# Two transformer blocks in one kernel: unread products in TensorE's waits, norm steps in another order, x loaded first

## The reference, cut to what matters

```python
for l in range(2):
    h = rms_norm(x, norm_mix[l])
    x = x + (short_conv_mixer(h, ...) if l == 0 else moba_attention(h, ...))
    x = x + mem_cross_attention(rms_norm(x, norm_mem[l]), rms_norm(mem, norm_memkv[l]), ...)
    x = x + swiglu(rms_norm(x, norm_ffn[l]), ffn_w_gu[l], ffn_w_down[l])
x = rms_norm(x, norm_final)
# second block
sh1, sc1, gt1, sh2, sc2, gt2 = split(silu(c) @ w_mod + b_mod)
h = rms_norm(x, g_mix) * (1 + sc1) + sh1
proj = h @ w_in          # gated delta net branch and latent attention branch
x = x + gt1 * (merged @ w_out)
h = rms_norm(x, g_ffn) * (1 + sc2) + sh2
x = x + gt2 * expert_choice_ffn(h, ...)   # 16 experts
out = rms_norm(x, g_final)
```

## Time and profile before

| what | value |
|---|---|
| runs | 1796.09, 1805.71 and 1807.78 us, median 1805.71 |
| profiled execution | 1801.72 us, its span 1800.0 us |
| TensorE busy | 1580.0 us (88%), 14736 products |
| VectorE, ScalarE, GpSimd busy | 868.8, 666.6, 145.5 us |
| mean PEclk | 0.93 |
| data moved by DMA | 417.17 MB |

### The profile page before, as it was taken

How to read it: one execution, slowest core, us unless ns; L and a number is a source line. 1 busy time by engine, 2 the same in 40 slices (tenths; PEclk the granted TensorE clock), 3 DMA queues, 4 the chain that set the end, 5 groups by cost and what they waited for, 6 DMA issues and landing times.

```text
span 1800.0 us, 35085 instructions
## 1 busy us (share of the span) xinstructions
PE 1580.0 (88%) x14736; PEld 1308.6 (73%) x14736; DVE 868.8 (48%) x1228; ACT 666.6 (37%) x869; POOL 145.5 (8%) x188
## 2 busy tenths in 40 slices
PE   7999999999999999999889799899898676666667
PEld 7999899988979889988888699698884232222223
DVE  4765466646565556664567588956541000000001
ACT  5445355434544445534465745524431000000001
POOL 5800000000000000000105002131010000000000
PEclk9999999999999999999899899999999677776789
DMA  7765656764736666755353154002779999999997
GB/s 240 237 211 188 187 161 190 236 244 152 258 114 219 197 185 188 195 173 192 102 165 94 55 164 135 26 27 95 275 290 402 421 421 421 421 421 421 420 421 306
DMA packets 254142, 417.17 MB, mean 232 GB/s; under 512 B 15103, under 2 KB 215346, under 8 KB 229426
## 3 DMA queue, kind: packets, MB, share of 16 engines
q1 hardware_dynamic: 252833, 411.96, 64.2%
q10 hardware_dynamic: 1168, 3.17, 0.5%
HBM read 414.04 MB, written 1.05 MB: 231 GB/s over the span
## 4 chain that ended last, share of the span: by engine, by line
issue 60%; PE 28%; DVE 4%; POOL 4%; ACT 3%; DMA 1%; DVEq 0%; POOLq 0%; ACTq 0%; SPq 0%
PE bank L417 3%; PE bank L418 3%; PE bank L419 3%; PE bank L1819 2%; PE bank L434 1%; PE bank L435 1%; PE bank L436 1%; PE bank L1036 1%; PE bank L1038 1%; POOL ang L867 1%; PE bank L1037 1%; DVE cy L1368 1%; ACT w_hi L243 1%; POOL ang L868 1%; PE bank L472 0%
## 5 line engine op out<-in xcount | busy, mean ns | idle before, releaser
L250 DVE TENSOR_TENSOR w_lo<-w_raw,w_hi 128x2048 fp32r<-128x2048 f32 (+2 forms) x178 | 401.5, 2258 | 258.0 <-ACT w_hi L243 257.9
L243 ACT ACTIVATE w_hi<-w_raw 128x2048 fp32r<-128x2048 f32 (+2 forms) x178 | 334.2, 1881 | 152.1 <-DMA w_raw<-in_ffn_w_down_dram 61.6
L417 PE MATMUL bank<-h_hi,w_hi 128*128 128x256 f32 x1168 | 327.5, 280 | 5.2 <-DVE h_lo L632 3.5
L418 PE MATMUL bank<-h_lo,w_hi 128*128 128x256 f32 x1168 | 325.8, 279 | 0.0
L419 PE MATMUL bank<-h_hi,w_lo 128*128 128x256 f32 x1168 | 325.6, 279 | 0.0
L2614 PE MATMUL bank<-w_exp,xeT 128*32 128x256 f32 x2048 | 174.3, 479 | 84.0 <-DMA w_exp<-in_w_up_dram 47.9
L417 PEld LDWEIGHTS bank<-h_hi,w_hi 128*128 128x128 f32 x1168 | 222.0, 190 | 7.0 <-issue 4.5
L419 PEld LDWEIGHTS bank<-h_hi,w_lo 128*128 128x128 f32 x1168 | 222.1, 190 | 0.0
L418 PEld LDWEIGHTS bank<-h_lo,w_hi 128*128 128x128 f32 x1168 | 221.7, 190 | 0.0
L2614 PEld LDWEIGHTS bank<-w_exp,xeT 128*32 128x32 f32 x2048 | 66.0, 129 | 185.2 <-DMA w_exp<-in_w_up_dram 83.3
L2782 DVE TENSOR_TENSOR hx<-sg,bank 128x256 f32<-128x256 f32 x16 | 6.7, 421 | 279.2 <-ACT sg L2756 279.2
(11 more groups left out here) (531 smaller groups left out, 3085.3 us busy)
## 6 DMA issues: line engine op xcount, KB each, us to landing
w_exp<-in_w_gate_dram SPq DMA_DIRECT2D x64, 1024.0 KB, 26.7
w_exp<-in_w_up_dram SPq DMA_DIRECT2D x64, 1024.0 KB, 26.9
w_exp<-in_w_down_dram SPq DMA_DIRECT2D x64, 1024.0 KB, 26.9
w_raw<-in_ffn_w_gu_dram SPq DMA_DIRECT2D x88, 512.0 KB, 5.0
w_raw<-in_w_in_dram SPq DMA_DIRECT2D x54, 512.0 KB, 4.7
w_mod<-in_w_mod_dram SPq DMA_DIRECT2D x24, 1024.0 KB, 7.6
w_raw<-in_ffn_w_down_dram SPq DMA_DIRECT2D x44, 512.0 KB, 4.3
w_raw<-in_mem_w_kv_dram SPq DMA_DIRECT2D x32, 512.0 KB, 4.7
```

The costliest lines, as they stand in the source:

```text
L243: e.activation(whi[slot][:, 0:w], raw[slot][:, 0:w], ACT.Copy).then_inc(S["hi_ready"], 1)
L250: e.tensor_tensor(wlo[slot][:, 0:w], raw[slot][:, 0:w], whi[slot][:, 0:w].bitcast(F32), ALU.subtract).then_inc(S["lo_ready"], 1)
L417: e.matmul(dst, whi[slot][:, lo:hi_], bh[:, k, :], start=(k == 0), stop=False)
L418: e.matmul(dst, whi[slot][:, lo:hi_], bl[:, k, :], start=False, stop=False)
```

## The change

- x is loaded by SP ahead of the first weights, not by ACT.
- The gains norm_mix are turned and copied ahead of the norm of x, not behind its transposes.
- Unread products are added to TensorE's list: 8 and 12 of the identity with itself around the turning of the gains, 5 behind the transposes of x, and 32 at the seam. Nothing reads their results.
- `fm_chunk`, in a chunk that waits for tiles, goes by tile k and takes both halves f for each, with one start for the bank.
- `load_late` goes from ACT's list to SP's, behind the sixth chunk of ffn(1).
- At the seam: sums are joined in another way (squares are scaled by 1/D as they are taken, the square of x of the last bank moves from VectorE to ScalarE and that of xn from ScalarE to VectorE), nrow is scaled in halves of 512 columns and the first eight transposes wait for the first halves only, and `split_biased` replaces the loop with two buffers by four buffers in x and another order of steps.

```diff
     def fm_chunk(bh, bl, width=256, kts=KT):
+        fs = width // P
         def chunk(e, c, u, slot):
-            for f in range(width // P):
+            by_tile = st.tiles is not None
+            for f, k in ([(f, k) for k in range(kts) for f in range(fs)] if by_tile else
+                         [(f, k) for f in range(fs) for k in range(kts)]):
                 dst = G[u][:, f * SEQ:(f + 1) * SEQ]
-                for k in range(kts):
-                    if f == 0:
-                        wait_tile(e, k)
...
+                begin = k == 0 and (f == 0 or not by_tile)
+                end = k == kts - 1 and (f == fs - 1 or not by_tile)
...
-    act.raw(load_x)
+    sp.raw(load_x)
...
+    def unread_identity(n):
+        def run(e):
+            e.wait_ge(*t_id)
+            for _ in range(n):
+                e.matmul(G[2][:, 0:P], ident[:, :], ident[:, :], start=True, stop=True)
+        pe.raw(run)
+    unread_identity(8)
+    t = pe.do(lambda e: e.transpose(G[3][:, 0:16], vrow[0:16, 0, :], ident[0:16, 0:16]), (mix_in, 16), t_id)
+    t_gain = dve.do(lambda e: e.tensor_copy(vcol[:, 0:16], G[3][:, 0:16]), t)
+    unread_identity(12)
     rows = norm_rows(x, [(x_in, 16)])
     first_split(0)
     turned = turn_rows(xn, rows)
-    t = pe.do(lambda e: e.transpose(G[3][:, 0:16], vrow[0:16, 0, :], ident[0:16, 0:16]), (mix_in, 16), t_id)
-    t_gain = dve.do(lambda e: e.tensor_copy(vcol[:, 0:16], G[3][:, 0:16]), t)
-    th = split_features(turned, lambda k: col("norm_mix", k), None, [t_gain])
+    unread_identity(5)
+    th = split_features(turned, lambda k: col("norm_mix", k), [t_gain])
     first_split(1)
...
         gemm(FT, source, fm_chunk(h_hi, h_lo), act_chunk=act_silu, dve_chunk=dve_gate, dve_links=2,
-             ready=[tx], act_ready=[tx], dve_ready=[tx])
+             ready=[tx], act_ready=[tx], dve_ready=[tx], beside={5: load_late} if l else None)
...
-    act.raw(load_late)
...
+    def split_biased(toks, gain, bias, free, whole):
...
+        by_dve(0)
+        by_dve(2)
+        hi(0)
+        by_act(1)
+        hi(1)
+        hi(2)
+        by_act(3)
+        hi(3)
+        for j in range(KT // 2):
+            tl = dve.do(lambda e, j=j: e.tensor_tensor(
+                h_lo[:, 2 * j:2 * j + 2, :], whole[:, j, :, :], h_hi[:, 2 * j:2 * j + 2, :].bitcast(F32), ALU.subtract), hi_at[j])
...
+    def unread_at_seam(n):
+        w = xfree[3]
+        def run(e):
+            e.wait_ge(*w)
+            for _ in range(n):
+                e.matmul(X[3][:, 0:SEQ], a_hi[:, 0, 0:P], a_hi[:, 1, :], start=True, stop=True)
+        pe.raw(run)
+    unread_at_seam(32)
```

More of the change, by code:

```diff
@@ L618, in turn_rows, with split_features @@
         return toks
-    def split_features(toks, gain, bias, free, also=(), into=None, behind=None, whole=None):
+    def split_features(toks, gain, free, into=None, behind=None):
         tls = []
@@ L625, in split_features @@
             tp = toks[j]
[L626 to L651, removed]
+            pair = [(2 * j + kk, X[j][:, kk * SEQ:(kk + 1) * SEQ]) for kk in range(2)]
+            for k, xj in pair:
+                th = act.do(lambda e, k=k, xj=xj: e.activation(to_hi[:, k, :], xj, ACT.Copy, scale=gain(k)),
+                            tp, *free, *([behind[k]] if behind else []))
+            for k, xj in pair:
+                tl = dve.do(lambda e, k=k, xj=xj: e.scalar_tensor_tensor(
+                    out=to_lo[:, k, :], in0=xj, scalar=gain(k), in1=to_hi[:, k, :].bitcast(F32),
+                    op0=ALU.mult, op1=ALU.subtract), th)
+            xfree[j] = tl
             tls += [tl, tl]
@@ L661, in norm_to_features @@
                 modulate(vector, j)
-        return split_features(turn_rows(xn, rows), gain, bias, free, whole=whole)
+        return split_features(turn_rows(xn, rows), gain, free)
     def attention(heads, kts, scale, score, v, pbuf, ptbuf, ready, causal=None, free=(), vector=None, beside=None):
@@ L1096, in build @@
     turned = turn_rows(xn, rows)
-    th = split_features(turned, lambda k: col("kv_norm", k), None, [all_used()])
-    th2 = split_features(turned, lambda k: col("norm_mix", 8 + k), None, [all_used()], into=h2,
+    th = split_features(turned, lambda k: col("kv_norm", k), [all_used()])
+    th2 = split_features(turned, lambda k: col("norm_mix", 8 + k), [all_used()], into=h2,
                          behind=tiles_of[th])
@@ new lines, in build @@
+    scaled = {}
+    for hf in range(2):
+        hs = slice(hf * BANK, (hf + 1) * BANK)
+        t0 = dve.do(lambda e, hs=hs: e.tensor_scalar(nrow[:, 0, hs], xn[:, 0, hs], roots[:, 2:3], None, ALU.mult), t_roots)
+        t1 = act.do(lambda e, hs=hs: e.activation(nrow[:, 1, hs], xn[:, 1, hs], ACT.Copy, scale=roots[:, 3:4]), t_roots)
+        scaled[2 * hf] = scaled[2 * hf + 1] = [t0, t1]
+    turned = turn_rows(nrow, [], by_pair=scaled)
+    ht4 = x[:, :, :].rearrange("p t d -> p (t d)").rearrange("p (j a t) -> p j a t", j=4, a=2)
@@ L1253, in build @@
+    th = split_biased(turned, lambda k: mcol[:, 1, k:k + 1], lambda k: mcol[:, 0, k:k + 1], [tcol, all_used()], ht4)
     dve.raw(lambda e, m=st.n + AHEAD - 1: lo_split(e, m, m % RING))
```

72 lines of the change are left out of this document (43 added, 29 removed).

## The result

The changed kernel takes 1798.3 us, median of 22 runs (1790.34 to 1803.29). The kernel before, run beside it, takes 1805.76, median of 22 (1796.09 to 1813.57). The ratio is 0.996, with a 95% interval of 0.9948 to 0.9972: 5.1 to 9.4 us are won. The forecast was 1791.5 with 14.2 won. So the direction is right, the time lies inside the range, and the size is about half of what was forecast.

A forecast was written before the change was run, and what follows sets the result against it. TensorE was taken to bound the first 1280 us, expert weights the span from 1360 on. Terms 4.8 + 3.8 + 5.4 + 0.2 = 14.2 off the median 1805.71 gave 1791.5, with 8 in 10 in 1782 to 1800.

The forecast's parts named there:

- The start, 4.8: Program start: x 1.2 earlier, gains 1.1 sooner, 2.5 from the clock held up; 4.8 us won, bounds 1.1 and 5.0.
- The clock was taken as 2.5: First chunk at the start: unread products keep TensorE at full clock, winning the 2.5 us between first and second chunk.
- the first rival, "the clock is down": Start and seam: both first products at 1.2 GHz; only 9.5 won, 1796.2; chance 0.27 with cases of only one down.
- Into ffn(1), 3.8: Entry of ffn(1): load_late off ScalarE's queue wins 2.9, no slow first products 0.9; 3.8 us, bounds 2.9 and 3.8.
- I cost it at nothing; the cover is these 6.7: Seventh weight chunk of ffn(1), behind the late loads on SP's queue: 6.7 us spare, so the delay costs nothing.
- Rival 3: ffn(1): broadcast loads, 8.0 each in a row, hold the weight queue; 17.3 stop, 3.1 slower, 1808.8; chance 0.03.
- its own counterargument: Against the held weight queue in ffn(1): the broadcasts' 8.0 us landings ran side by side, with weights beside them.
- The seam, 5.4: Between the blocks: less idle, faster transposes, first product 1.0 sooner, no 1.34 stop; 5.4 us won, bounds 1.0 and 5.6.
- By tile elsewhere, 0.2: Chunks outside start and seam: waits for low parts leave at most 0.6 between pairs; 0.2 us taken as won.
- rival 2: First block: the start's gain is lost there, VectorE hardly pausing between 70 and 100 us; 9.4 won, 1796.3; chance 0.08.

The follow-up runs named there:

- e2: Changed kernel with 12 unread products instead of 5 behind the first 16 transposes; 1790.62 in one run (before 1799.35).
- e4: Changed kernel with the five late loads spread behind chunks 5, 8, 11 and 14 of ffn(1); 1801.15 in one run (before 1799.35).
- e8: Changed kernel with late loads spread over ffn(1) and 12 unread products instead of 5 ahead of the first product; 1799.2, ratio 0.9968.
- e3: Changed kernel without the 32 unread products at the seam; 1796.67 in one run (before 1799.35).
- e5: Changed kernel with the chunks of products by output half again, not by tile; 1798.11, ratio 0.9969.
- f1: Kernel before with only the five late loads moved to SP's queue behind chunk 5 of ffn(1); 1802.31, ratio 0.9999.
- e6: Changed kernel with the five late loads on ScalarE's queue again, ahead of its norm in ffn(1); 1798.17, ratio 0.996.
- e7: Changed kernel with x loaded first on ScalarE's queue again; 1793.87 in one run.
- f2: Kernel before with only the new start: x on SP's queue, gains turned before the norm, 8, 12 and 5 unread products; 1800.74, ratio 0.998.
- e1: Changed kernel without the 25 unread products ahead of the first chunk; 1799.44 in one run (before 1799.35).

## Why the prediction was right or wrong

The direction is right, and so is the mechanism at each of the four places: each shows there. The sum of 14.2 is too high, and the time came within the range with about half of the gain that was forecast. In means over the table's traces:

- **The start, 4.8.** Measured: 23.83 in the mean for the 49th with the old start (four traces), 21.03 with the new one and five unread products (six traces): 2.8. Two terms of it were mis-sized. x came 0.74 sooner where I took 1.2 (0.5 in the mean of all traces), and the gains 1.1 as forecast: 14.15 became 14.6. The unread products were priced at 0.23 each from transposes; one took 0.25 to 0.46, and the twelve ended at 8.69 and not near 7. In the trace of after that cost nothing; in e2, e4 and e8 the first eight held VectorE's half of the norm 0.15 to 0.35 behind ScalarE's, and the first product came no later. The clock was taken as 2.5, the difference of two chunks in one trace. The old start lost 2.6 in that trace (8.05 for the chunk) but 1.6 in the second (7.25, with a pace of 5.65), and the new one loses some 1.5 in half of its traces. So the first rival, "the clock is down", came half true at the start, and not at all at the seam.
- **Into ffn(1), 3.8.** 16.35 in the mean of five traces, 12.96 of nine: 3.4.
- **"I cost it at nothing; the cover is these 6.7".** This step failed, in its size. The chunk was not issued late, it landed late: 1.5 MB ahead of it on the same queue took the DMAs, and its halves needed 8.6 and 11.6 us instead of 5.0. Behind the landing come not two splits, 2 x 2.29 = 4.6, but ScalarE's table load of 1.28, then 1.92 and 2.29: 5.5 from 692.81 to 698.34. The second half landed 7.0 later than priced (11.6 behind an issue 0.4 later, less 5.0), which uses up the spare (6.7, or 7.3 at the pace of 5.65), and the table load, which the sum left out, is more than the stop of 0.9. It cost 1.0 and 0.8 in two traces of seven, 0.3 in the mean. Rival 3 asked for the 8.0 of each broadcast in a row; they ran side by side (7.1 and 7.0), as its own counterargument had it.
- **The seam, 5.4.** 18.62 in the mean of four traces, 14.00 to 14.02 in all that have the whole part: 4.6. The trace of before that I read was one of the two dear ones (19.02 and 19.63; the other two are 17.96 and 17.86). The idle, the transposes, the stop and the order are as forecast; 1.1 is the unread products' (e3), 1.3 the order by tile (e5). Against the forecast 49th, 13.55 behind the last product, the changed kernel's 14.00 is 0.45 late: the first product 0.2 (+8.28 instead of +8.1), and its chunk takes 5.7 instead of 5.45.
- **By tile elsewhere, 0.2.** At most 0.2 in ffn(1).

So these marks give 2.8 + 3.4 - 0.3 + 4.6 = 10.5 where I had 14.2. The run gives 7.5, with 5.1 to 9.4. For the 1.1 to 5.4 that are left three things stand in the table, and none is shown to be the cause.

- The middle, the largest, to which the prediction gave nothing outside rival 2: 638.3 in the mean of the ten traces with the new start, 636.0 in the four with the old, 2.3 more, with single traces between 633.9 and 641.7. All traces have the same 5037 products there. Set beside the shortest time that each product took in any of the traces, the pace costs 3.0 more with the new start, falls of the clock 1.1 less, and other waits some 0.5 more.
- The body: its first chunks have the pace of 5.44 in four of the five traces that enter ffn(1) behind the long gap and the low clock (180.26 four times, 184.74 once, mean 181.2), but in only two of the nine that enter it by the short gap (mean 183.2). Of this 2.1 some 0.2 is the stop that is already counted; 1.9 is pace. It would make the late loads' gain of 3.4 small, as both f1 and e6 have it. But in ffn(0), which all traces enter by the same short gap, nine of fourteen have 5.44, so the short gap alone doesn't set it.
- The rest behind the seam is 924.1 in the mean with the old seam (four traces) and 924.8 with the new one (ten), 0.7 more, with single traces between 921.4 and 926.7.

All three would bring 10.5 to 5.6, at the lower end of what the runs give. So what the marks promise and the runs don't give is in these traces mostly the pace of 5.65, which is commoner with the new start and behind the short gap. With so few traces that can be luck, and what sets the pace stays open; the order by tile doesn't, since e5 has the pace of 5.65 without it.

The prediction's method has a fault that the sum hides: it took the marks of one trace as properties of the kernel. Its start (24.51) was 0.7 and its seam (19.02) 0.4 above the means of four traces with the same code, and the chunk's 2.5 of clock was taken whole.

## What to carry to other kernels

A mark in one trace tells what a change does at its place, not what the run gains: with 4.5 us between equal loops of two executions, a change worth 3 us needs marks from several traces, marks that leave no stretch of the span out, and more than 12 timed runs. To keep a queue's next load in time it isn't enough that it is issued in time; count the bytes issued right ahead of it. Unread products in a wait can keep the clock up; whether they do so more surely the less idle time they leave behind them (a fall in none of two traces against three of six here) is not shown. They can delay what stands behind them on TensorE (e7), and what waits for that.

## What the runs showed of the hardware

- The pace. At PEclk 1.00 and with TensorE fully busy, 48 products of 256 columns take 5.44 or 5.65 us, and one of the two can hold for a loop of 110 us. From the 49th product of the program to the end of the down projection it accounts for 5 to 17 us in a trace (the sum of what each product of 256 columns took over 0.1133).
- The clock also falls where the busy time shows no gap. A row and two windows of e8:

```profile
442.93 3.62 PE L1104 MATMUL bank<-kT,swap 32*32 32x512 f32 x8
```

```profile
446.00:447.00 1.00, 1.00 (x6) 0.53 (x5) 1.00 (x3) 0.00 (x0) 0.00 (x0) 1.00 0.00 0
448.00:450.00 2.00, 2.00 (x11) 2.00 (x11) 1.97 (x2) 0.00 (x0) 0.00 (x0) 0.50 0.00 0
```

  TensorE is called busy throughout, but ahead of the fall it ran eight small products (weights of 32x32), one in 0.43 us or more, and the products of 256 columns go from 0.113 to 0.213 us at 447.04, 0.56 behind the last of them. Each trace has eight such products at two places, near 450 us (kT with swap) and 500 us (qT with swap); at 17 of the 28 places a fall begins 0.2 to 0.7 us behind their end. Two other falls in the first block, near 94 us in f2 and 515 us in f1, follow an idle time of 1.82. In after, e1 and e3 the clock stayed up behind the same small products, so they are not enough for a fall. The falls cost 0 to 5.1 us in the first block behind the start; the trace of after had none, that of before two of 1.7 us.
- An unread product of 128x128 in fp32 leaves two records and takes 0.25 us (2.94 / 12), 0.42 (4.98 / 12) or, for the first eight of the program, 0.46 (3.65 / 8), where I had taken 0.23.
